# The block scheme of the output projection from the third output tile on, with three weight chains and reordered input sums

## The reference, cut to what matters

```python
for i in range(DEPTH):
    hn = _rmsnorm(h, norm_g[i])
    u = hn @ w_in[i]
    ...
    ya = ya * jax.nn.silu(a_z)                      # (512, 1024)
    yb = _window_attention(...) * jax.nn.silu(b_z)  # (512, 1024)
    h = h + jnp.concatenate([ya, yb], axis=-1) @ w_out[i]
    e = _rmsnorm(p[i] @ w_pe[i], pe_g[i])
    h = h + e * jax.nn.sigmoid(h @ w_pg[i])
```

## Time and profile before

| | us |
|---|---|
| median of 3 runs (lowest, highest) | 2547.13 (2545.57, 2547.58) |
| the profiled execution | 2547.91 |
| its span in the profile | 2545.9 |
| busy: PE, its weight loads, DVE, POOL, ACT | 2530.1, 2122.1, 1482.9, 1359.1, 1037.8 |
| granted clock, mean over the span | 0.998 |

### The profile page before, as it was taken

The page is one execution under the profiler, slowest core; times in us unless marked ns, Lnnn a source line. Parts: engine busy times, 40 slices in busy tenths (PEclk is TensorE's granted clock), DMA queues, the critical chain, the costliest instruction groups (busy, mean ns, idle before and its releaser), DMA issues.

```text
span 2545.9 us, 40237 instructions
## 1 busy us (share of the span) xinstructions
PE 2530.1 (99%) x14832; PEld 2122.1 (83%) x14832; DVE 1482.9 (58%) x2426; ACT 1037.8 (41%) x1584; POOL 1359.1 (53%) x1716
## 2 busy tenths in 40 slices
PE   9999999999999999999999999999999999999999
PEld 7888888889988888888887899888888888888887
DVE  7877766574462387777665754634654655522622
ACT  6222365543362341223655434634323656323521
POOL 6555545442355555555444424555666777655554
PEclk9999999999999999999999999999999999999999
DMA  8333344248633333333433586243333333433332
GB/s 257 104 99 95 95 128 113 92 161 187 155 105 126 116 118 98 99 99 100 111 113 98 173 181 158 91 132 116 109 99 128 98 96 100 141 96 93 99 92 106
DMA packets 92821, 303.96 MB, mean 119 GB/s; under 512 B 9168, under 2 KB 25296, under 8 KB 89616
## 3 DMA queue, kind: packets, MB, share of 16 engines
q1 hardware_dynamic: 76128, 271.60, 33.5%
q0 software_dynamic: 6912, 25.17, 5.7%
q10 hardware_dynamic: 9648, 5.36, 1.0%
HBM read 288.43 MB, written 16.81 MB: 120 GB/s over the span
## 4 chain that ended last, share of the span: by engine, by line
PE 96%; DMA 2%; DVE 1%; issue 0%; ACT 0%; POOL 0%; DVEq 0%; ACTq 0%
PE acc L1825 19%; PE acc L1826 19%; PE acc L1827 19%; PE sc L1825 6%; PE sc L1826 6%; PE sc L1827 6%; PE sc L2095 1%; PE sc L2096 1%; PE sc L2097 1%; PE acc L1849 1%; PE sc L1849 1%; PE acc L1851 1%; PE sc L1851 1%; PE sc L1855 1%; PE acc L1855 1%; DMA a<-in_w 1%
## 5 line engine op out<-in xcount | busy, mean ns | idle before, releaser
L669 POOL TENSOR_TENSOR WL<-raw,WH 128x256 fp32r<-128x256 f32 x1600 | 1267.8, 825 | 967.2 <-ACT WH L715 966.9
L1825 PE MATMUL acc<-XH,WH 128*128 128x512 f32 x2128 | 831.1, 391 | 0.0
L1826 PE MATMUL acc<-XL,WH 128*128 128x512 f32 x2128 | 828.4, 389 | 0.0
L1827 PE MATMUL acc<-XH,WL 128*128 128x512 f32 x2128 | 828.0, 389 | 0.0
L715 ACT ACTIVATE WH<-raw 128x1024 fp32r<-128x1024 f32 x402 | 424.1, 1058 | 917.4 <-PE acc L1827 653.4
L1825 PEld LDWEIGHTS acc<-XH,WH 128*128 128x128 f32 x2128 | 399.4, 188 | 87.4 <-issue 4.5
L1827 PEld LDWEIGHTS acc<-XH,WL 128*128 128x128 f32 x2128 | 399.5, 188 | 83.7
L1826 PEld LDWEIGHTS acc<-XL,WH 128*128 128x128 f32 x2128 | 399.5, 188 | 81.9
L1825 PE MATMUL sc<-XH,WH 128*128 128x512 f32 x640 | 249.0, 389 | 0.0
L1826 PE MATMUL sc<-XL,WH 128*128 128x512 f32 x640 | 249.0, 389 | 0.0
L1827 PE MATMUL sc<-XH,WL 128*128 128x512 f32 x640 | 249.0, 389 | 0.0
(11 more groups left out here) (355 smaller groups left out, 3796.1 us busy)
## 6 DMA issues: line engine op xcount, KB each, us to landing
raw<-in_w SPq DMA_DIRECT2D x420, 512.0 KB, 3.6
a<-in_w POOLq DMA_DIRECT2D x24, 512.0 KB, 6.4
raw<-in_w POOLq DMA_DIRECT2D x24, 512.0 KB, 6.5
a<-in_w SPq DMA_DIRECT2D x18, 512.0 KB, 6.7
h_spill<-H SPq DMA_DIRECT2D x8, 1024.0 KB, 6.2
H<-h_spill SPq DMA_DIRECT2D x8, 1024.0 KB, 6.6
a<-bias_band SPq DMA_DIRECT2D x16, 384.0 KB, 4.1
H<-in_x SPq DMA_DIRECT2D x5, 1024.0 KB, 7.2
```

The costliest lines, as they stand in the source:

```text
L669: part = pool.tensor_tensor(WL[:, c], raw[:, c], WH[:, c].bitcast(F), ALU.subtract)
L1825: pe.matmul(bank, WH[:, c], xh, start=first, stop=False)
L1826: pe.matmul(bank, WH[:, c], xl, start=False, stop=False)
L1827: return pe.matmul(bank, WL[:, c], xh, start=False, stop=last)
```

## The change

It sets `PLAIN` to 2, so that seven pairs (49 steps in place of 42) go through the block scheme and four ring units less through the plain one. Of that follow a new `STEPS_OF`, in which p1 and p2 of the first two pairs come first and the steps of up to three pairs alternate; a third place for chain a (a0, a1, a2) and a third "x" bank; ring slots that jump by one at steps 12, 24 and 36; low parts of the steps 0 to 3 on POOL as well as those of p2 (`SIDE_LOWS`). The input sums are made in another order: all four differences for S1 first (`diff`), then S3, from that S2, from that S4, group by group, with the fourth group inside the loop of the steps. SP loads seven places at once behind the last plain unit's low part. The diff, cut to its core:

```diff
--- before.py
+++ after.py
...
-PLAIN = 4
+PLAIN = 2
...
 STEPS_OF = (
-    ("p1", 0), ("p2", 0), ("p5", 0), ("p3", 0), ("p1", 1), ("p6", 0), ("p2", 1), ("p7", 0), ("p5", 1), ("p4", 0), ("p3", 1), ("p6", 1),
-    ("p1", 2), ("p7", 1), ("p2", 2), ("p5", 2), ("p4", 1), ("p3", 2), ("p6", 2),
+    ("p1", 0), ("p2", 0), ("p1", 1), ("p2", 1), ("p5", 0), ("p1", 2), ("p6", 0), ("p5", 1), ("p3", 0), ("p6", 1), ("p2", 2),
+    ("p5", 2), ("p7", 0), ("p3", 1), ("p4", 0), ("p7", 1), ("p6", 2), ("p3", 2), ("p4", 1),
     ("p1", 3), ("p7", 2), ("p2", 3), ("p5", 3), ("p4", 2), ("p3", 3), ("p6", 3),
-    ("p1", 4), ("p7", 3), ("p2", 4), ("p5", 4), ("p4", 3), ("p3", 4),
-    ("p1", 5), ("p6", 4), ("p3", 5), ("p5", 5), ("p7", 4), ("p6", 5), ("p4", 4), ("p7", 5), ("p2", 5), ("p4", 5))
+    ("p1", 4), ("p7", 3), ("p2", 4), ("p5", 4), ("p4", 3), ("p3", 4), ("p6", 4),
+    ("p1", 5), ("p7", 4), ("p2", 5), ("p5", 5), ("p4", 4), ("p3", 5),
+    ("p1", 6), ("p6", 5), ("p3", 6), ("p5", 6), ("p7", 5), ("p6", 6), ("p4", 5), ("p7", 6), ("p2", 6), ("p4", 6))
+SIDE_LOWS = [j for j, (kind, q) in enumerate(STEPS_OF) if kind == "p2" or j < RING]
 FAST_N = len(STEPS_OF)
 STEP_AT = {step: j for j, step in enumerate(STEPS_OF)}
...
 def fast_slot(j):
 
-    return (j if j < FAST_N // 2 else j + 2) % RING
+    return (j + (j >= 12) + (j >= 24) + (j >= 36)) % RING
...
 def bank_of(kind, q):
 
-    return {"p2": "v", "p3": "v", "p5": "z"}.get(kind, "x%d" % (q % 2))
+    return {"p2": "v", "p3": "v", "p5": "z"}.get(kind, "x%d" % (q % 3))
...
-        S1B, S2B, S3B = VB, N, TR[0]
-        XB_OF = {"x0": SC[0], "v": SC[1], "z": G[0], "x1": G[1]}
-        PLACES = (("a0", a2, 2), ("b0", a2, 1), ("c0", a2, 0), ("b1", raw, 0), ("c1", raw, 1), ("a1", raw, 2))
+        S1B, S2B, S3B = (VB, N), (VB, N), TR[0]
+        XB_OF = {"x0": G[0], "v": G[1], "x1": SC[0], "z": SC[1], "x2": TR[1]}
+        PLACES = (("a1", a2, 2), ("b1", a2, 1), ("c1", a2, 0), ("a2", raw, 0), ("b0", raw, 1), ("c0", raw, 2), ("a0", raw, 3))
...
-                pair_units(u0, OUT0, OUT0 + RING, skip)
...
                 sp.wait_ge(pv_done, ly * CT + CT)
-                load_place("a0", block_unit(ly, 0, 0, 0))
-                load_place("c0", block_unit(ly, 0, 1, 0))
+                sp.wait_ge(wl_ready, u0 + PE0)
+                for q in range(2):
+                    load_place("a%d" % q, block_unit(ly, q, 0, 0))
+                    load_place("c%d" % q, block_unit(ly, q, 1, 0))
                 load_place("b0", block_unit(ly, 0, 1, 1))
-                sp.wait_ge(wl_ready, u0 + OUT0 + RING + 3)
-                load_place("a1", block_unit(ly, 1, 0, 0))
-                load_place("c1", block_unit(ly, 1, 1, 0))
+                load_place("a2", block_unit(ly, 2, 0, 0))
                 load_place("b1", block_unit(ly, 1, 1, 1))
-                sp.wait_ge(s4_low, 4 * ly + 4)
-                for c in range(2, 4):
-                    if ly:
-                        sp.wait_ge(h_out[c], ly * 16)
-                    h_dma(c, False, ly == 0)
-                sp.wait_ge(wl_ready, u0 + PE0)
-                load(u0 + (PE0 + 3 + skip + SKIP_U), 3)
                 for j, (kind, q) in enumerate(STEPS_OF):
                     if kind not in ("p2", "p4", "p7"):
                         continue
+                    if (kind, q) == ("p2", 2):
+                        sp.wait_ge(s4_low, 4 * ly + 4)
+                        for c in range(2, 4):
+                            if ly:
+                                sp.wait_ge(h_out[c], ly * 16)
+                            h_dma(c, False, ly == 0)
                     sp.wait_ge(*low_made(ly, j))
-                    if q + 2 < FOURS:
-                        load_place(place_of(kind, q), block_unit(ly, q + 2, 0 if kind == "p4" else 1, 1 if kind == "p7" else 0))
+                    following = q + CHAIN_PLACES[CHAIN_OF[kind][0]]
+                    if following < FOURS:
+                        load_place(place_of(kind, q), block_unit(ly, following, 0 if kind == "p4" else 1, 1 if kind == "p7" else 0))
                     elif (kind, q) == ("p2", FOURS - 2):
                         sp.dma_start(praw, pin[bass.ds(ly, 1)].rearrange("a p n -> (a p) n")).then_inc(p_in, 16)
-                    elif q == FOURS - 1:
-                        n = {"p7": 0, "p2": 1, "p4": 2}[kind]
+                    elif (kind, q) in (("p7", FOURS - 1), ("p2", FOURS - 1), ("p4", FOURS - 2), ("p4", FOURS - 1)):
+                        n = {"p7": 1, "p2": 2, "p4": 3 * (q == FOURS - 1)}[kind]
                         load(u0 + (PE0 + n + skip + SKIP_U), n)
...
                 for j, (kind, q) in enumerate(STEPS_OF):
-                    if kind == "p2":
+                    if j in SIDE_LOWS:
...
+                def diff_high(c):
+                    act.wait_ge(comb_ready, 16 * ly + c + 1)
+                    act.activation(sums_of(1, False)[:, 2 * c:2 * c + 2, :], two(S1B[c % 2]), ACT.Copy).then_inc(comb_high, 1)
+
                 def comb_highs(c):
-                    n = 4 * (4 * ly + c)
-                    for which, count, bank in ((1, 2, S1B), (3, 3, S3B), (2, 4, S2B)):
+                    n = 16 * ly + 4 + 3 * c
+                    for which, count, bank in ((3, 2, S3B), (2, 3, S2B[c % 2])):
                         act.wait_ge(comb_ready, n + count)
                         act.activation(sums_of(which, False)[:, 2 * c:2 * c + 2, :], two(bank), ACT.Copy).then_inc(comb_high, 1)
+
+                def last_high(c):
+                    act.wait_ge(comb_ready, 16 * ly + 4 + 3 * c + 3)
+                    act.activation(sums_of(4, False)[:, 2 * c:2 * c + 2, :], att_half(c, 0), ACT.Copy).then_inc(s4_high, 1)
...
                     act.wait_ge(*landed(ly, kind, q))
                     if slot_before(j) is None:
-                        act.wait_ge(w_used, u0 + (OUT0 + RING + fast_slot(j) + 1))
+                        act.wait_ge(w_used, u0 + (OUT0 + fast_slot(j) + 1))
...
-                comb_highs(0)
-                prep(u0, OUT0)
-                prep(u0, OUT0 + 1)
-                comb_highs(1)
-                prep(u0, OUT0 + 2)
-                prep(u0, OUT0 + 3)
-                comb_highs(2)
-                comb_highs(3)
+                diff_high(0)
                 fast_prep(0)
                 fast_prep(1)
-                for c in range(4):
-                    act.activation(sums_of(4, False)[:, 2 * c:2 * c + 2, :], att_half(c, 0), ACT.Copy).then_inc(s4_high, 1)
-                for j in range(2, FAST_N):
+                for c in range(1, 4):
+                    diff_high(c)
+                comb_highs(0)
+                fast_prep(2)
+                fast_prep(3)
+                comb_highs(1)
+                comb_highs(2)
+                fast_prep(4)
+                for c in range(3):
+                    last_high(c)
+                fast_prep(5)
+                comb_highs(3)
+                last_high(3)
+                for j in range(6, FAST_N):
                     fast_prep(j)
...
+                def diff(c):
+                    if c >= 2:
+                        dve.wait_ge(comb_low, 12 * ly + c - 1)
+                    dve.tensor_tensor(two(S1B[c % 2]), att_half(c, 1), y_half(c, 1), ALU.subtract).then_inc(comb_ready, 1)
+
+                def diff_low(c):
...
                 def comb_adds(c):
-                    n = 4 * (4 * ly + c)
-                    dve.tensor_tensor(two(S1B), att_half(c, 1), y_half(c, 1), ALU.subtract).then_inc(comb_ready, 1)
+                    n = 16 * ly + 4 + 3 * c
+                    dve.wait_ge(comb_low, 12 * ly + 4 + 2 * c)
+                    dve.tensor_tensor(two(S3B), y_half(c, 0), y_half(c, 1), ALU.subtract).then_inc(comb_ready, 1)
                     dve.wait_ge(comb_ready, n + 1)
-                    stt(two(S2B), two(S1B), -1.0, y_half(c, 0), ALU.mult, ALU.subtract).then_inc(comb_ready, 1)
-                    dve.tensor_tensor(two(S3B), y_half(c, 0), y_half(c, 1), ALU.subtract).then_inc(comb_ready, 1)
+                    stt(two(S2B[c % 2]), two(S3B), -1.0, att_half(c, 1), ALU.mult, ALU.subtract).then_inc(comb_ready, 1)
                     dve.wait_ge(comb_ready, n + 2)
-                    stt(att_half(c, 0), two(S2B), -1.0, att_half(c, 0), ALU.mult, ALU.subtract).then_inc(comb_ready, 1)
+                    stt(att_half(c, 0), two(S2B[c % 2]), -1.0, att_half(c, 0), ALU.mult, ALU.subtract).then_inc(comb_ready, 1)
...
+                diff(0)
                 for c in range(4):
-                    if c:
-                        dve.wait_ge(comb_low, 3 * (4 * ly + c))
-                    comb_adds(c)
-                    comb_lows(c)
+                    if c < 3:
+                        diff(c + 1)
+                    diff_low(c)
+                comb_adds(0)
+                comb_lows(0)
+                comb_adds(1)
                 add_out(0)
                 add_out(1)
-                fast_lows(0)
-                fast_lows(1)
-                for c in range(4):
```

(33 more changed lines are left out.)

33 lines of the change are left out of this document (22 added, 11 removed).

## The result

The changed kernel takes 2564.8 us (median of 4 runs, 2562.25 to 2568.7). Beside it on the same chip the kernel before took 2547.36 us. The ratio is 1.0073, 95% interval 1.0057 to 1.0089: **slower by 17.4 us**, on the interval by 15 to 23. The prediction was 2563.0 us, in a range of 2548 to 2577, and slower with a chance of 0.76. The profiled execution took 2566.28 us, with a span of 2564.5.

A forecast was written before the change was run, and what follows sets the result against it. PE's own instructions and waits were taken as the bound. Per layer, 163.3 us of work + 7.9 + 3.5 + 1.0 + 3.2 + 1.0 = 179.9 us, +15.1 over two layers: 2563.0 us, range 2548 to 2577.

The forecast's parts named there:

- start, to step 3: Block stage's start: input sums under two plain tiles end late and POOL holds DVE; 7.9 us a layer (5.4 to 9.5).
- steps 4 to 9: Low part 7 comes late and its accumulating DMA lands slowly, 20.8 us against PE's 17.3; 3.5 us a layer.
- step 10: Its high part follows step 9's on ACT and its low part takes POOL 2.8; 1.0 us more a layer.
- ring jump: At step 12: low part 15 awaits low 13's DMA ahead of the addition freeing step 14's bank; 3.2 us a layer.
- slow clock, edges of waits: PE drops to 1.2 GHz behind waits; only the stretch behind step 14's counted, 1.0 us a layer (0 to 1.9).
- The bound: Whole kernel: time is PE's own instructions plus its few microseconds of waiting; PE busy 2530.1 us, 99% of the span.
- ports don't hold: Rival at the start: a POOL group costs DVE 0.5 us at most, start costs 5.4; 2558 us, chance 0.17.
- so I take 8.1: Steps 4 to 9: landing time entered for low part 7's accumulating DMA, with 2 MB of H issued just before.
- What goes: Pair 5's waits go with a third chain buffer and third "x" bank; nothing late in the rest of the stage.
- DMA pile-up: Rival: accumulating DMAs queue behind seven loads and H, steps 0 to 2 wait too; 2574 to 2582 us, chance 0.13.
- all covered: Rival: only the work is left, 163.3 us a layer, old losses vanish; 2529.8 us, chance 0.14.
- nets out: Rival: new losses equal the old plus the 1.9 gained, 8.6 to 9.8 us a layer; 2547.9 us, chance 0.10.

The follow-up runs named there:

- x1: Changed kernel with ScalarE making the high parts of all four differences before the weights' high parts 0 and 1; 2554.5 us, 1.0031 to before.
- x3: Changed kernel with POOL issuing the accumulating DMAs of steps 0 and 2 behind the low parts of steps 1 and 3; 2557.7 us.
- x2: Changed kernel with VectorE making the additions to H of steps 0 and 1 before group 2 of the input sums; 2564.9 us.
- x6: Changed kernel with ScalarE's differences first and VectorE's low parts 11 and 15 behind the additions of steps 8 and 12; 2545.4 us, 1.0001 to before.
- x4: Changed kernel with VectorE making low part 15 behind the addition of step 12, not ahead of it; 2560.7 us, 1.0054 to before.
- x8: Changed kernel with the ring's first jump at step 20 in place of 12; 2560.3 us, 1.0054 to before.
- x5: Changed kernel with the order moves of x1 and x4 together; 2547.6 us, 1.0010 to before.
- x10: Changed kernel with differences first, low parts 11 and 15 behind additions, step 7's parts and DMA before step 6's, first jump at 20; 2542.6 us.

## Why the prediction was right, point by point

The sum and the trace, in us per layer; the measured ones are idleness of the profile in the two layers:

| term | predicted | measured |
|---|---|---|
| start, to step 3 | 7.9 | 8.1, 7.0 |
| steps 4 to 9 | 3.5 | 0, 0.3 |
| step 10 | 1.0 | 2.3, 2.35 |
| ring jump | 3.2 | 2.3, 2.2 |
| slow clock, edges of waits | 1.0 | 5.4, 6.0 |
| loss | 16.6 | 18.1, 17.8 |

**The bound, right.** PE's own work plus its waits is all there is: the plain tiles took 21.9 us in each layer, and the rest of the program moved by 1.3 us.

**The start, right in mechanism and sum, its two parts mis-sized.** High parts 0 and 1 ended at 540.5 and 541.7 (541.4 and 542.7 predicted), VectorE idled 4.2 us (some 6), and the differences ended at 545.3 (546.0). x1, which takes order and holds out together, shows that most of it starts there. The split of the 7.9 was 5.4 for the chain and 2.5 for the port. x3 takes the port's part away and leaves 4.1 us of gaps before steps 2 and 3 in the first layer, 2.8 in the second. So the port costs over 4 us at the start, the upper end of its range, and the chain 2.8 to 4.1 where 5.4 was entered. The rival "ports don't hold" falls: the two subtractions lost 2.1 and 2.6 us. Its price was sound, since x3, in which they lose 0.5 at most, runs at 2557.7 (2558 predicted).

**Where the prediction named VectorE's queue, half right.** It had the addition of step 1 "behind" group 2 and low part 4. That is what PE waited for, but x2 shows that taking it out of the queue gains nothing.

**Steps 4 to 9, wrong: the step that failed is "so I take 8.1".** Low part 7 ended 10.3 us behind the addition (10.4 predicted), but its DMA landed 5.9 us after issue, near the median of the earlier trace rows, not like the ones behind H loads. That takes 2.2 us off. ScalarE's high part 9, which that landing releases:

```profile
580.05 1.06 ACT L944 ACTIVATE WH<-a 128x1024 fp32r<-128x1024 f32 x1 [7.70 <-DMA a<-in_w]
```

What is left of the 3.5 lies behind the slow clock of step 3, which delays PE by 1.6: the waits behind "take that in", as the prediction had it, and step 9 started 0.2 us after its low part was ready.

**Step 10, wrong mechanism, larger.** The prediction had its low part late behind step 9's. It was the bank: low part 11 held by the port, ahead of the addition that frees it. The same hold that the prediction priced at the start was not looked for here, though step 10's low part is POOL's and follows on the DMA issue of step 9. x6 shows the price: 1.5 us of gap, and 2.2 us of the time in both layers together. The predicted term was there, hidden under the bank's wait: the 1.0 us of gap left in x6 is a wait for POOL's low part.

**Ring jump, right, one term a little large.** 2.3 and 2.2 us for 3.2, because the DMA took 5.4 us where 6.4 was entered; x4 and x8 confirm the place and the way.

**Clock, half right: the step that failed is that only the slow stretch behind step 14 counts.** In the first layer steps 3, 10 and 14, behind the three long waits, took 1.6, 1.5 and 1.3 us longer than the 2.88 of a step at the full clock, and step 15 another 0.3. Step 3's 1.6 hides most of the DMA's wait, as said above, and the 1.6 of steps 14 and 15 stand where the prediction had 1.0. But step 10's 1.5 counts as well, since the chain that sets step 14 starts when PE leaves the slot of step 10. About 0.7 more are the edges of the waits.

So the nearness of 2564.8 to 2563.0 is in part luck, two errors of opposite sign. Step 9 started 10.2 and 9.9 us late where the sum has 11.4, so 1.2 and 1.5 too much. Step 10 with its clock added 3.9 and 4.0 where it has 1.0. The jump with its clock came to 4.0 and 3.9 for 4.2.

**What goes, right.** Pair 5's waits are gone and no wait over 0.2 us stands in pairs 3 to 6. That the third buffers do it, as the prediction had it, is not shown: the order of the steps changed with them in every run. Nor is the last pair far from a wait: in x3, x4, x5, x6 and x10 up to 0.8 us stand before its step 45.

**DMA pile-up, all covered and nets out** fell. PE waited before step 2 only for POOL's low part, the accumulating DMAs on the chain landed 5.9 and 5.4 us after issue, not 10, and the queues of VectorE and POOL made every long wait. PE idled 8.1 and 7.0 us up to step 3, which neither "all covered" nor "nets out" has room for.
